# Order of the attention heads in the two later layers of a four-layer kernel

## What is computed

```python
def window_gqa(q, k, v, kc, vc, sink):            # 4 heads of 64, keys within 128 tokens, and a sink
    s_loc = where(valid, q @ k_band, NEG_INF)
    p = softmax(concatenate([s_loc, s_ctx, s_sink]))
def neighbourhood_attn(q, k, v, kc, vc, rpb):     # 4 heads of 64, a bias by place
    s_loc = q @ k * scale + bias
    p = softmax(concatenate([s_loc, s_ctx]))
def diff_weights(q, k, v, lam):                   # 4 heads, two maps of width 32 each
    s = einsum('bqhmd,bkhmd->bhmqk', q, k) * (32 ** -0.5)
    p = softmax(s)
    w = p[:, :, 0] - lam * p[:, :, 1]
    return w @ v
```

## Time and profile before

| | us |
|---|---|
| median of 3 runs | 3886.86 (3877.76 to 3894.97) |
| the profiled execution | 3877.81 |
| its span from the first to the last instruction | 3875.8 |
| pairs stage of layer 2 in it | 2058.50 to 2320.30 |
| pairs stage of layer 3 in it | 3232.86 to 3436.30 |

### The profile page before, as it was taken

One profiled execution on the slowest core, in us unless ns is written; L12 is line 12 of the kernel. 1 busy time (PEld: TensorE's weight loads), 2 busy tenths in 40 slices (PEclk: granted clock), 3 DMA queues, 4 the chain that ended last, 5 costly groups with the idle time before them and its releaser, 6 DMA issues. The chain is left out here.

```text
span 3875.8 us, 44999 instructions
## 1 busy us (share of the span) xinstructions
PE 3509.9 (91%) x17200; PEld 2652.4 (68%) x17200; DVE 1637.7 (42%) x3029; ACT 1091.4 (28%) x1382; POOL 1323.7 (34%) x919
## 2 busy tenths in 40 slices
PE   6997999999787799999987788999999997989998
PEld 5863788878576678886564336888899474347887
DVE  5433333357445556562613432744355504532111
ACT  2243322233311332222112333222344102343222
POOL 2314444444544243432002453344400001563443
PEclk8998999999898899999996998999999996999999
DMA  5510344422100034441110001435354120012221
GB/s 219 201 69 12 120 162 158 159 96 97 44 1 1 22 119 150 159 157 65 55 65 1 1 1 55 152 136 194 136 174 168 62 75 1 1 44 83 96 91 67
DMA packets 54936, 355.54 MB, mean 92 GB/s; under 512 B 5888, under 2 KB 6912, under 8 KB 19456
## 3 DMA queue, kind: packets, MB, share of 16 engines
q1 hardware_dynamic: 54496, 351.35, 24.8%
q10 hardware_dynamic: 288, 2.10, 0.1%
HBM read 351.33 MB, written 2.10 MB: 91 GB/s over the span
## 5 line engine op out<-in xcount | busy, mean ns | idle before, releaser
L383 POOL TENSOR_TENSOR W_LO<-ring,W_HI 128x2048 fp32r<-128x2048 f32 (+1 forms) x177 | 729.7, 4122 | 1092.0 <-ACT W_HI L371 1092.0
L439 PE MATMUL PS<-H_HI,W_HI 128*128 128x512 f32 (+1 forms) x1888 | 712.9, 378 | 32.1 <-DVE H_LO L818 23.6
L441 PE MATMUL PS<-H_HI,W_LO 128*128 128x512 f32 (+1 forms) x1888 | 703.0, 372 | 0.0
L440 PE MATMUL PS<-H_LO,W_HI 128*128 128x512 f32 (+1 forms) x1888 | 702.5, 372 | 0.0
L371 ACT ACTIVATE W_HI<-ring 128x2048 fp32r<-128x2048 f32 (+1 forms) x214 | 366.2, 1711 | 481.5 <-PE PS L429 443.7
L439 PEld LDWEIGHTS PS<-H_HI,W_HI 128*128 128x128 f32 x1888 | 359.5, 190 | 96.1 <-issue 32.0
L441 PEld LDWEIGHTS PS<-H_HI,W_LO 128*128 128x128 f32 x1888 | 358.8, 190 | 63.0
L440 PEld LDWEIGHTS PS<-H_LO,W_HI 128*128 128x128 f32 x1888 | 359.6, 190 | 59.5 <-issue 0.2
L860 DVE SCALAR_TENSOR_TENSOR PS<-ring,SC,PS 128x256 f32<-128x256 f32 x768 | 376.2, 490 | 27.0
L427 PE MATMUL PS<-HID_HI,W_HI 128*128 128x512 f32 (+1 forms) x880 | 325.3, 370 | 4.9 <-DVE W_LO L383 4.0
L429 PE MATMUL PS<-HID_HI,W_LO 128*128 128x512 f32 (+1 forms) x880 | 323.7, 368 | 0.0
(11 more groups left out here) (317 smaller groups left out, 5419.2 us busy)
## 6 DMA issues: line engine op xcount, KB each, us to landing
ring<-w_tiles SPq DMA_DIRECT2D x273, 1024.0 KB, 4.8
ring<-d_tiles SPq DMA_DIRECT2D x80, 704.0 KB, 4.1
X<-xT SPq DMA_DIRECT2D x1, 2048.0 KB, 12.6
WORK<-rope_tables ACTq DMA_DIRECT2D x2, 1024.0 KB, 7.1
outT<-H SPq DMA_DIRECT2D x8, 256.0 KB, 2.2
CN<-consts SPq DMA_DIRECT2D x1, 1379.0 KB, 16.4
X<-ctxT SPq DMA_DIRECT2D x1, 1024.0 KB, 9.4
PR<-params SPq DMA_DIRECT2D x1, 465.5 KB, 3.6
```

The lines of the kernel that those rows point to most:

```text
L383: eng.tensor_tensor(W_LO[:, b, 0:w], ring[:, g % SLOTS, 0:w], W_HI[:, b, 0:w].bitcast(F32), ALU.subtract).then_inc(sig("tile_split"), 1)
L439: pe.matmul(to, hi[:, cols(k, j)], x_hi(k), start=k == 0, stop=False)
L440: pe.matmul(to, hi[:, cols(k, j)], x_lo(k), start=False, stop=False)
L441: mm = pe.matmul(to, lo[:, cols(k, j)], x_hi(k), start=False, stop=k == n - 1)
```

## The change

`mixer_tasks` makes the same tasks in another order: before W0, W1, N0, N1, D00, D01, D10, D11; now D00, D01, D10, D11, N0, N1, W0, W1 (in layer 2 each still followed by its context task). `dve_pairs` gets one more instruction: where a task's units have more rows than those of the task before, MAXIMA is set to zero ahead of its `rows`, with a wait until that is done (`chain`). That is so once in each of the two layers, at N0. The first layer's tasks (`causal_tasks`) are not touched.

```diff
+        def unit_rows(task):
+            return task["units"][0]["rows"].stop - task["units"][0]["rows"].start
...
                 if n:
                     dve.wait_ge(sig("pair_maxima_read"), b_r + n)
+                if p and unit_rows(tasks[p - 1]) < unit_rows(task):
+
+                    chain(dve.memset(MAXIMA, 0.0))
                 for u, unit in enumerate(task["units"]):
...
+            for n in range(2):
+                for m in range(2):
+                    q_steps = [dict(products=[(i, 0, T, 0)], reads=[(0, 1, T, 0, i, None)]) for i in range(NT)]
...
+            for n in range(2):
+                q_steps, steps = [], []
+                for i in range(NT):
+                    bias = lambda u, i=i, n=n: BT[:, 2 * n + u, 6 - 2 * i:14 - 2 * i, :].rearrange("p s c -> p (s c)")
...
             for heads in ((0, 3), (1, 2)):
...
                 both([window_unit(h) for h in heads], 1.0, q_steps + context_steps(), steps, [window_out(h) for h in heads])
-            for n in range(2):
-                q_steps, steps = [], []
...
-            for n in range(2):
-                for m in range(2):
...
```

More of the change, by code:

```diff
@@ L2434, in diff_unit @@
                             lambda c: V2[:, c, h * 64:h * 64 + 64])
+            for n in range(2):
+                for m in range(2):
+                    q_steps = [dict(products=[(i, 0, T, 0)], reads=[(0, 1, T, 0, i, None)]) for i in range(NT)]
+                    steps = [plain_step(c, 0, T) for c in range(6)]
+                    both([diff_unit(2 * n + u, m) for u in range(2)], 32 ** -0.5, q_steps + context_steps(), steps,
+                         [(slice(0, P), H[:, 4 + n, :])], minus=SM[:, 42:43] if m else None)
+            for n in range(2):
+                q_steps, steps = [], []
+                for i in range(NT):
+                    bias = lambda u, i=i, n=n: BT[:, 2 * n + u, 6 - 2 * i:14 - 2 * i, :].rearrange("p s c -> p (s c)")
+                    q_steps.append(dict(products=[(i, 0, T, 0)], reads=[(0, 1, T, 0, i, bias)]))
+                    turned = lambda u, i=i, n=n: BT_TURNED[:, 2 * n + u, (3 - i) * P:(7 - i) * P]
+                    steps.append(plain_step(i, 0, T, bias=turned))
+                steps += [plain_step(4, 0, T), plain_step(5, 0, T)]
+                both([neighbour_unit(2 * n + u) for u in range(2)], 1.0, q_steps + context_steps(), steps,
+                     [(slice(0, P), H[:, 6 + n, :])])
             for heads in ((0, 3), (1, 2)):
```

## The result

| | before | after |
|---|---|---|
| median of 7 runs each, us | 3882.57 (3871.56 to 3894.97) | 3912.02 (3905.14 to 3913.52) |
| ratio of the times | | 1.0073, 95% interval 1.0054 to 1.0092 |
| the profiled execution | 3877.81 | 3905.14 |
| its span | 3875.8 | 3903.2 |
| pairs stage of layer 2 | 261.8 | 268.7 |

The changed kernel is slower by 0.73%, about 28 us. The forecast was +13 (0.34%). The time lies in the stated range, but on the side of rival A: slower, and by more than 0.5%. Of the 27.4 us between the spans, layer 2's stage has 6.9, layer 3's 19.7, and everything else 0.8.

The account below looks back on a forecast made before the run. The prediction took PE, busy for 91% of the span, as the bound. Layer 2's +11.3, layer 3's +1.5 and the memset's 0.5 made +13 us; on the median of 3886.9 this gave 3900, range 3878 to 3925.

Parts of the forecast that it names:

- rival A: First D tasks, layers 2 and 3: half speed stays, as 32-row steps don't bring the clock back; +37 us, 3924; chance 23%.
- The likeliest case: Whole kernel: time within 0.5% of the kernel before, given 0.61.
- The start: Stage start up to the first exponent: four wider items add 3.9 us per layer, 25.1 us; right if 24.5 to 25.5.
- The first task at half speed: D00 in each layer: somewhat more than two half-speed steps at 3.0 us each, +7, hence 36 us.
- I leave that out of the new one.: Layer 3: old D00's 17.00 us at half speed, which cost 10 us against D01, is not priced in the new order.
- add 10 us: Layer 3 after the first task: no 17 us stretch at half speed; if one comes back, add 10 us.
- four more: Rival A's size: four more half-speed steps in each layer beyond about two, 8 x 3.0 = 24 us.
- Rival B: First task D00: a densely busy PE brings full speed at once; no change, 3887; chance 18%.
- Rival C: Layer 2, N1 and W0: one-item steps cost 22 us each and full speed comes at once; -10 us, faster; chance 7%.
- Layer 2: Pairs stage of layer 2: places priced by the nearest old place, sum 273.1 us against 261.8, so +11.3.
- POOL's surplus: W1, last in each stage: POOL's greater work adds 4.4 us in layer 2 and 1.7 us in layer 3.
- The memset: Ahead of N0's rows: DVE's memset with its wait costs 0.25 us, twice 0.5; upper end 2.4 in all.

Follow-up runs that it names:

- nomask_last: The changed kernel without POOL's masks in the last window task of each stage; 1.0061 of the time of the kernel before.
- p_dwn: The changed kernel with the W tasks moved between D and N (order D W N); 1.0018 of the time of the kernel before.
- rows64_before: The kernel before, old order, with both maps' score matmuls on 64 rows instead of 32; 0.9992 of the time of the kernel before.
- warm_before: The kernel before with filler matmuls on 128 rows behind the six maxima items ahead of the first scores, both later layers; 0.9986, repeated 0.9991.

## Why the prediction was right and wrong

Right were the sign, the range and the kind of cause: the places of the tasks, not the amount of work. The likeliest case, within 0.5%, did not come; the forecast was 15 us too low. What it gave to the starts and first tasks, +17.4 us in both layers together, came out at +18.5. The rest of the two stages was to get 4.6 us shorter and got 8.1 us longer, and there the terms of layer 3 failed.

| layer 3 | predicted | measured | difference |
|---|---|---|---|
| start | 25.1 | 24.0 | -1.1 |
| D00 | 36 | 40.4 | +4.4 |
| D01 | 18.5 | 27.1 | +8.6 |
| D10 | 19.0 | 19.1 | +0.1 |
| D11 | 21.3 | 27.4 | +6.1 |
| N0, N1 | 43.3 | 40.9 | -2.4 |
| W0 | 20.0 | 21.9 | +1.9 |
| W1 and end | 21.7 | 22.3 | +0.6 |

- **The start.** Right in layer 2 (24.99). In layer 3 it took 24.04 and not 24.5 to 25.5, since its first 2.2 us were at full speed.
- **The first task at half speed.** I let the clock come back after somewhat more than two steps, as in W0. In layer 3 it came back behind the last exponent of D00 (0.51), so all six steps were slow. In layer 2 it came back at 2109.60, 26 of the 33.76 us in and just ahead of the scores of the last step: five slow steps. They cost only 4.6 us over the 29.13 at full speed, where 3.0 for each would be 15. So both the number of slow steps and their price were wrong, in opposite directions, and the near hit of the term (33.76 for 36) is luck; so is the sum of the two layers, with -2.2 in one and +4.4 in the other. In layer 3 a step with two items took 7.75 us at half speed, not the 6.05 of one item.
- **"I leave that out of the new one."** The sentence on the 17.00 us is the step that failed most. It was evidence of how D tasks can behave at any place, and I treated it as an accident of one. D01 and D11 had such pieces (0.75 and 0.88) and brought 14.7 of the 18.3 us that layer 3 went over its forecast. The sign named for it, add 10 us if such a stretch comes back, would have given +23.
- **Rival A** had the mechanism: 32-row steps don't bring the clock back. By one of its signs (D01's clock below 0.8) it holds in layer 3 (0.75) and not in layer 2 (0.94); by the other, D00 above 42 us, it just misses (40.44). It put "four more" steps at 3.0 us in each layer; the slow steps of layer 2 came too but cost about a third of that, so its 3924 was too high and 3912 lies between it and the forecast. What speaks for it was in hand: 17.00 busy us out of 17.00 at 0.50.
- **Rival B** falls. Its rule, activity releases the throttle, is that of the Trainium skill, page TensorE: Matmul & The Clock Gate, section What's actually happening; the trace here disagrees for 32-row matmuls: 13.70 of 13.70 us, 20.50 of 20.50 and, with fillers, 24.56 of 25.52 busy, all at 0.50. With 64-row items and fillers the trace agrees with it (full speed after 6.34 us).
- **Rival C**, items win: N1 and W0 in layer 2 were cheaper than forecast (25.90 and 25.62 for 27.2 and 26.9), not the 22 that it needed.
- **Layer 2** came out 4.5 us below its forecast: D00 2.2 less, N1 and W0 1.3 each, N0 0.7, D11 1.7 more. D01 and D10 (30.20, 30.48 for 30.6), the start (24.99 for 25.1) and W1 with its end (29.96 for 30.0) were as priced. Pricing a place by the old place with the same neighbours worked where the clock was the same in both.
- **POOL's surplus** was right and nomask_last confirms it. That PE would wait for a mask was named as a thing that would prove me wrong; it happened (2.04 us) but inside the 22.3 us that had been priced by POOL's work.
- **The memset** cost nothing that shows:

```profile
L1298 DVE MEMSET WORK<- x2: 165/165/165, 2201.6 to 3363.9; 128x128 f32 x2
```

165 ns both times, as at the stage's start. The stall that I took as the upper end, 2.4 us for the two, does not show. The first memset began when POOL was idle and tests nothing, but the second began in the middle of a POOL add:

```profile
3363.73 1.26 POOL L1429 TENSOR_TENSOR SUM_REST<-SUM_REST,BIG 128x512 f32<-128x512 f32 x1 [2.56 <-ACT BIG L1388]
3363.87 0.17 DVE L1298 MEMSET WORK<- 128x128 f32 x1
3364.07 1.02 DVE L1305 SCALAR_TENSOR_TENSOR WORK<-WORK 128x4 f32<-128x4 f32 x2
```

The stall is there, one instruction later. The pair at L1305, whose inputs are two pieces of WORK, took 1.02 us and its first one ended with the add; at N0 of layer 2, with POOL idle, the same pair took 0.23 us. The Trainium skill's page SBUF — State Buffer, section SBUF: two separate sides, says that a GpSimd instruction that reads SBUF and a VectorE instruction in a two-port mode or with two inputs in SBUF can't hold the shared ports together. The trace agrees for L1305. The memset has no input, and pricing it by L1330, which reads two tensors, was the mistake. The kernel before has the pair at L1299 as well, so this is no cost of the change.

**What stays open.** Why the clock falls in one D task and not in the next is not settled: D10 of layer 3 ran at 1.00 in the change and at 0.75 in p_dwn, and D01 the other way round, with the same rows. The orders differ in luck as well as in rule, and the exact size of the loss (0.73% here, 0.18% in p_dwn) comes from these pieces. A version that keeps the two maps apart and whose D scores stand on 64 rows (one map's queries with zeros in the other's rows) was not tried. By rows64_before it would win nothing in the old order. None of the twelve runs gave an order or version whose gain over the kernel before is confirmed: warm_before had 0.9986 with an interval below 1, and its repetition had not.

## What to carry to other kernels

Read the granted clock of each stretch before pricing a moved piece of work: a duration holds only at the clock that it was taken at, and a piece at half speed with PE fully busy says something of the work in it and may come back wherever that work goes. Where a stage begins at half speed, as here, the work whose matmuls use more rows is the better first one, with 32-row matmuls (also those of the next task, worked ahead) kept out of the first steps. Last should stand the task with the least left for the slowest engine to finish, here not the one with masks on POOL.

## What the hardware showed that was not expected

- TensorE stayed at 1.2 GHz through stretches in which it had no idle time at all: 13.70, 20.50 and 17.00 us with 32-row matmuls in them. The changed kernel with 64 rows for D (rows64_after) was at 2.4 GHz 27.2 us into each stage, with PE busy for only 17.1 of these.
- With filler matmuls on 128 rows between 64-row items full speed came after 6.3 us, when two of them had run. Between 32-row items all six brought nothing: the clock was up only 51 us into the stage of layer 2.
- Dips begun in D tasks last longer (mean 10.0 us of 43) than those begun in W tasks (6.3 us of 24).
- At 1.2 GHz a step's score matmuls took 1.92 us in place of 1.13, but the stage lost less: a line through the runs of the table gives about 0.3 us of stage for each us at half speed. The orders differ in other things too, so that is a rough figure.
- A DVE instruction with two inputs in SBUF stood still until POOL's add had ended (945 ns in place of about 160), and a memset in the middle of the same add did not (165 ns).
